# The FFN pre-norm of the next 512 tokens moved into the up-projection loop of the current 512

## The reference, cut to what matters

```python
def rmsnorm(x, g):
    y = x * lax.rsqrt(jnp.mean(x * x, axis=-1, keepdims=True) + EPS)
    return y * g

for l in range(DEPTH):
    h = rmsnorm(x, norm_mix_pre[l])
    proj = h @ w_in[l]
    # retention in chunks of 128 tokens (4 heads) -> y_ret
    # short gated convolution (3 taps)            -> y_sc
    # GLU, convolution of 31 taps, layernorm      -> y_cf
    merged = gates[:, :, 0] * y_ret + gates[:, :, 1] * y_sc + gates[:, :, 2] * y_cf
    x = x + rmsnorm(merged @ w_o[l], norm_mix_post[l])

    h = rmsnorm(x, norm_ffn_pre[l])
    up = causal_dwconv(h @ w_up[l], ffn_conv_w[l])       # 3 taps, per channel
    gate, val = jnp.split(up, 2, axis=-1)
    f = (jax.nn.silu(gate) * val) @ w_down[l]
    x = x + rmsnorm(f, norm_ffn_post[l])
```

## Time and profile before

| | |
|---|---|
| median of 3 runs | 3403.17 us (3396.67 to 3809.15) |
| the profiled execution's own time | 3395.79 us |
| its span, first to last instruction, slowest core (core 6) | 3394.3 us |
| spans of the 8 cores | 3382.3 to 3394.3 us |
| granted TensorE clock, mean over the span | 0.899 to 0.902 |
| PE busy | 2760.2 us, 81% |
| DVE busy | 1414.1 us, 42% |
| ACT busy | 1030.6 us, 30% |
| POOL busy | 151.2 us, 4% |
| DMA queue of POOL, share of the 16 engines | 31.3% |

### The profile page before, as it was taken

The page is one execution under the profiler, slowest core; times in us unless marked ns, Lnnn a source line. Parts: engine busy times, 40 slices in busy tenths (PEclk is TensorE's granted clock), DMA queues, the critical chain, the costliest instruction groups (busy, mean ns, idle before and its releaser), DMA issues.

```text
span 3394.3 us, 41546 instructions; the slowest of 8 cores (3382.3 to 3394.3 us)
## 1 busy us (share of the span) xinstructions
PE 2760.2 (81%) x12476; PEld 1257.4 (37%) x12724; DVE 1414.1 (42%) x4445; ACT 1030.6 (30%) x1825; POOL 151.2 (4%) x290
## 2 busy tenths in 40 slices
PE   3688796697897979898966879777879796979797
PEld 1333343343343434343432324333324343434343
DVE  3423445424454343434343334553334543434343
ACT  1421322422223232323234132323132332323232
POOL 0000000000001000000000000000000010101010
PEclk9899897798898989898977979888989898989898
DMA  6030333030427552525231204231114292626251
GB/s 177 16 54 13 76 66 70 2 67 1 87 49 125 87 87 50 89 49 94 52 72 21 47 13 92 38 72 35 33 37 81 44 167 58 112 51 106 56 100 44
DMA packets 51274, 219.60 MB, mean 65 GB/s; under 512 B 5104, under 2 KB 5360, under 8 KB 43888
## 3 DMA queue, kind: packets, MB, share of 16 engines
q0 software_dynamic: 41184, 187.71, 31.3%
q1 hardware_dynamic: 9872, 29.21, 2.6%
HBM read 396.21 MB, written 8.39 MB: 119 GB/s over the span
## 4 chain that ended last, share of the span: by engine, by line
PE 71%; DVE 11%; issue 7%; ACT 6%; DMA 3%; DVEq 0%; SPq 0%; ACTq 0%; POOLq 0%
PE PSF L402 70%; ACT arena L384 4%; DVE arena L387 2%; DVE arena L396 2%; DVE arena L391 2%; DMA RING<-wst 1%; PE PSB L406 1%; DVE RS L396 1%; ACT HT L384 1%; DVE arena L411 1%; DMA PVt<-pv 1%; DMA out<-X 1%; DVE SMALL L599 1%; ACT SMALL L410 1%; DVE SMALL L411 0%
## 5 line engine op out<-in xcount | busy, mean ns | idle before, releaser
L402 PE MATMUL PSF<-HT,RING 128*128 128x512 bf16 x6016 | 1418.1, 387 | 72.9 <-ACT arena L384 33.0
L384 ACT ACTIVATE arena<-PSF 128x512 bf16<-128x512 f32 (+2 forms) x1024 | 610.2, 597 | 1533.2 <-PE PSF L402 1236.3
L402 PE MATMUL PSF<-arena 128*128 128x512 bf16 (+2 forms) x3796 | 859.9, 372 | 167.3 <-DVE arena L387 68.8
L402 PEld LDWEIGHTS PSF<-HT,RING 128*128 128x128 bf16 x6144 | 608.3, 99 | 825.9 <-issue 130.3
L387 DVE TENSOR_TENSOR arena<-PSF,arena 128x512 f32<-128x512 f32 (+1 forms) x592 | 403.3, 690 | 679.4 <-PE PSF L402 447.4
L402 PEld LDWEIGHTS PSF<-arena 128*128 128x128 bf16 (+1 forms) x3868 | 368.2, 98 | 614.3 <-issue 189.3
L391 DVE TENSOR_SCALAR arena<-CST,PVt 128x128 bf16<-128x128 f32 x1600 | 330.5, 279 | 68.0 <-PE PSF L402 68.0
L406 PE MATMUL PSB<-IDB,arena 128*128 128x128 bf16 x704 | 94.6, 298 | 300.3 <-DVE arena L391 243.9
L356 POOL DMA_DIRECT2D RING<-wst x264 | 139.5, 529 | 3166.6 <-PE PSF L402 1501.1
L399 DVE COPY FH<-arena 128x2 bf16<-128x2 bf16 x352 | 60.5, 172 | 375.0 <-ACT arena L384 373.8
L402 PE MATMUL PSF<-arena,RING 128*128 128x512 bf16 x752 | 196.0, 380 | 0.8
(11 more groups left out here) (49 smaller groups left out, 845.1 us busy)
## 6 DMA issues: line engine op xcount, KB each, us to landing
RING<-wst POOLq DMA_DIRECT2D x192, 512.0 KB, 5.5
RING<-wst POOLq DMA_DIRECT2D x32, 1152.0 KB, 8.3
RING<-wst POOLq DMA_DIRECT2D x24, 1024.0 KB, 7.9
RING<-wst POOLq DMA_DIRECT2D x16, 768.0 KB, 6.4
arena<-wst POOLq DMA_DIRECT2D x22, 512.0 KB, 9.7
X<-x SPq DMA_DIRECT2D x4, 2048.0 KB, 20.6
arena<-rope SPq DMA_DIRECT2D x16, 512.0 KB, 8.5
out<-X SPq DMA_DIRECT2D x4, 2048.0 KB, 7.0
```

Source lines behind the costliest of these rows:

```text
L384: S.op("act", lambda e: e.activation(out=out, in_=in_, func=func, **kw), r, w)
L402: S.pe([(lambda e, o=o, a=a, b=b, s0=s0, s1=s1: e.matmul(o, lhsT=a, rhs=b, start=s0, stop=s1)) for (o, a, b, s0, s1) in specs], r, w)
```

## The change

The diff does these things:

1. `HT` is used as two halves of 512 tokens, in turn: quarter q lies in half q % 2.
2. The FFN's `prenorm` becomes `ffn_stats(q)` (four Squares into a scrap tile `JUNK`, mean and epsilon, Sqrt, reciprocal, results in `PST`) and `ffn_apply(q)`. The latter works in two pairs of token tiles through `HN2`, a buffer of two tiles: two DVE multiplications, then for each of the 8 channel blocks two transposes into a `PSB` bank and one move of 256 columns into `HT`.
3. Quarter 0's stats and apply stand ahead of the loop over quarters. Those of quarter qt + 1 are emitted in quarter qt's up loop, at j = 6 (stats) and j = 13 (apply), each ahead of `up_front(j + 1)`.
4. The arena's push and pop around each quarter are gone, and with them the barrier at each quarter's end; the buffers are allocated once. `slR`, the Silu result, is bf16 instead of fp32.
5. In `ret_front` each PSUM tile has a fixed bank (0: value, 1: gate, 2 and 3: scores, 4 and 5: output, 2 again: the state update) instead of the rotation's next one.
6. The `AR.pop()` and `AR.push()` between the retention and the short convolution are gone, with the barrier.

```diff
-    def pf():
+    def pf(fixed=None):
+        if fixed is not None:
+            return PSF[:, fixed, :], "pf%d" % fixed
...
-                pv_, pvr = pf()
+                pv_, pvr = pf(0)
...
-                pg, pgr = pf()
+                pg, pgr = pf(1)
...
-                psA, psAr = pf()
-                psB, psBr = pf()
+                psA, psAr = pf(2)
+                psB, psBr = pf(3)
...
-                poA, poAr = pf()
-                poB, poBr = pf()
+                poA, poAr = pf(4)
+                poB, poBr = pf(5)
...
-                    pkv, pkvr = pf()
+                    pkv, pkvr = pf(2)
...
-            AR.pop()
             if l == 0 and hf == 0:
                 DBG("ART", ART, ["art0", "art1"])
-            AR.push()
...
+        HN2 = AR.alloc([2, 1024], BF16)
...
+        slR = Rot("sl", [512], BF16)
...
+        def ffn_stats(q):
+            sl_ = (q % 2) * 16
+            for a in range(4):
+                tt = q * 4 + a
+                ACT(JUNK[:], X[:, tt, :], AF.Square, ["x%d" % tt], ["junkp", "fss%d" % (q % 2)],
+                    accum_out=PST[:, sl_ + a:sl_ + a + 1])
+            TS(PST[:, sl_ + 4:sl_ + 8], PST[:, sl_:sl_ + 4], 1.0 / D, EPS, ALU.mult, ALU.add, ["fss%d" % (q % 2)], ["fms%d" % (q % 2)])
+            POW(PST[:, sl_ + 8:sl_ + 12], PST[:, sl_ + 4:sl_ + 8], ["fms%d" % (q % 2)], ["frs%d" % (q % 2)])
+
+        def ffn_apply(q):
+            sl_ = (q % 2) * 16
+            g = q % 2
+            for pair in range(2):
+                for a2 in range(2):
+                    a = pair * 2 + a2
+                    tt = q * 4 + a
+                    TS(HN2[:, a2, :], X[:, tt, :], PST[:, sl_ + 8 + a:sl_ + 9 + a], None, ALU.mult, None,
+                       ["x%d" % tt, "frs%d" % (q % 2)], ["hn2_%d" % a2])
+                for kc in range(8):
+                    p, pr = pb()
+                    TR([(p[:, a2 * 128:(a2 + 1) * 128], HN2[:, a2, kc * 128:(kc + 1) * 128]) for a2 in range(2)],
+                       ["hn2_0", "hn2_1", "idb"], [pr])
+                    dst = HT[:, kc, g * 512 + pair * 256:g * 512 + (pair + 1) * 256]
+                    res = ["ht%d_%d_%d" % (kc, g, pair)]
+                    if kc % 2 == 0:
+                        ACT(dst, p[:, 0:256], AF.Copy, [pr, "pv"], res, scale=PV[:, PV_FFNPRE + kc:PV_FFNPRE + kc + 1])
+                    else:
+                        TS(dst, p[:, 0:256], PV[:, PV_FFNPRE + kc:PV_FFNPRE + kc + 1], None, ALU.mult, None, [pr, "pv"], res)
+
+        ffn_stats(0)
+        ffn_apply(0)
         for qt in range(4):
-            AR.push()
-            HNv = ACTT[:, 0:8, :].rearrange("p a b -> p (a b)").rearrange("p (t d) -> p t d", d=1024)
-            prenorm(l, [qt * 4 + a for a in range(4)], PV_FFNPRE, HT, HNv, lambda i: ["actt%d" % (2 * i), "actt%d" % (2 * i + 1)])
...
+            hg = qt % 2
+            HTq = HT[:, :, hg * 512:(hg + 1) * 512]
+            htr = ["ht%d_%d_%d" % (kc, hg, pr_) for kc in range(8) for pr_ in range(2)]
...
             for j in range(NFF):
                 wd_maybe(j)
+                if qt < 3 and j == 6:
+                    ffn_stats(qt + 1)
+                if qt < 3 and j == 13:
+                    ffn_apply(qt + 1)
                 nctx = up_front(j + 1) if j + 1 < NFF else None
...
-            AR.pop()
         AR.pop()
```

More of the change, by code:

```diff
@@ L321, in build @@
     SM_ = nc.alloc_sbuf_tensor("SMALL", [128, 64], F32)
+    PST = nc.alloc_sbuf_tensor("PST", [128, 32], F32)
+    JUNK = nc.alloc_sbuf_tensor("JUNK", [128, 1024], BF16)
     PSF = nc.alloc_psum_tensor("PSF", [128, 6, 512], F32)
@@ L816, in build @@
         ACTT = AR.alloc([NFF, 512], BF16)
+        HN2 = AR.alloc([2, 1024], BF16)
+        UGR = Rot("ug", [514], BF16)
+        UVR = Rot("uv", [514], BF16)
+        DGF = Rot("dgf", [6, 128], BF16)
+        slR = Rot("sl", [512], BF16)
+        tmpR = {"junk": AR.alloc([512], BF16), "t": Rot("pnt", [512], F32, 2)}
         S.dma("sp", lambda e, l=l: e.dma_start(out=GBC[:], in_=gbc_d[l, 1]), "gbc", writes=["gbc"])
         wd_issued = 0
-        for qt in range(4):
-            AR.push()
-            HNv = ACTT[:, 0:8, :].rearrange("p a b -> p (a b)").rearrange("p (t d) -> p t d", d=1024)
-            prenorm(l, [qt * 4 + a for a in range(4)], PV_FFNPRE, HT, HNv, lambda i: ["actt%d" % (2 * i), "actt%d" % (2 * i + 1)])
[L823 to L827, removed]
+        def ffn_stats(q):
[6 more added lines that the diff above has]
+            POW(PST[:, sl_ + 8:sl_ + 12], PST[:, sl_ + 4:sl_ + 8], ["fms%d" % (q % 2)], ["frs%d" % (q % 2)])
@@ L842, in up_front @@
                 pg_, pgr_ = pf()
-                MM([(pg_, W[:, kc, 0:128], HT[:, kc, 0:512], kc == 0, kc == 7) for kc in range(8)], htr + [wr], [pgr_])
+                MM([(pg_, W[:, kc, 0:128], HTq[:, kc, :], kc == 0, kc == 7) for kc in range(8)], htr + [wr], [pgr_])
                 pv2, pv2r = pf()
-                MM([(pv2, W[:, kc, 128:256], HT[:, kc, 0:512], kc == 0, kc == 7) for kc in range(8)], htr + [wr], [pv2r])
+                MM([(pv2, W[:, kc, 128:256], HTq[:, kc, :], kc == 0, kc == 7) for kc in range(8)], htr + [wr], [pv2r])
                 ACT(ug[:, 2:514], pg_, AF.Copy, [pgr_], [ugr])
@@ L881, in build @@
                 DBG("ACTT", ACTT, ["actt%d" % j for j in range(NFF)])
-            tmpR = {"junk": AR.alloc([512], BF16), "t": Rot("pnt", [512], F32, 2)}
             for a in range(4):
```

## The result

| | before | after |
|---|---|---|
| median of 10 runs | 3402.5 us | 3327.1 us |
| ratio, after to before | | 0.9771 (95%: 0.9753 to 0.9790) |
| span of the profiled execution, slowest core | 3394.3 us | 3323.6 us |
| span of core 6 in both | 3394.3 us | 3320.6 us |
| granted TensorE clock | 0.899 to 0.902 | 0.911 to 0.913 |

The change made the kernel faster by 2.3%; forecast were 3342 us and 1.8%, with a range of 3316 to 3376.

What follows compares the result with a forecast made beforehand. PE, busy 81% of the span, was taken as the bound, with time to gain where it idles or runs at the lower clock. -157.0 + 96.0 + 5.0 - 5.6 = -61.6 us from 3403.2 gave 3342 us, range 3316 to 3376.

Steps and rivals of the forecast that it cites:

- The boundaries: Six quarter ends in the FFN: PE's idle time, transposes and cold matmuls there all go, -157.0 us.
- The stop in step 13: Apply at j = 13 of the up loop: PE loses 12.5 us a quarter to products, transposes and moves (bounds 11.5, 15.1).
- The clock: Up matmuls behind the stop in step 13: lower PE clock loses 2.1 us a quarter (bounds 0 and 2.9).
- The stats: Squares and Sqrt at j = 6 of the up loop: PE held up 1.4 us a quarter (bounds nothing and 4.2).
- the cost in the loop: Moved pre-norm in the up loop: 1.4 + 12.5 + 2.1 = 16.0 us a quarter, times six 96.0.
- Quarter 0: Pre-norm ahead of each layer's quarter loop, now in two pairs: +2.5 us each, +5.0 in all.
- Retention barriers: Barrier between retention and short convolution removed: 1.4 us, four times, -5.6 us.
- Retention chunks: Fixed PSUM banks in the retention: nothing gained; a clock shift of 16 us at most, in either direction.
- the cheaper stop: Rival on the up loop: clock may stay at 1.00, stats may hide; 12.5 us a quarter, 3321 us total; 26%.
- The dearer stop: Rival on the up loop: rounds at 1.52 us and half the stats' upper bound; 20.8 us a quarter, 3371 total; 13%.
- The boundary did not stay in part: Rival at quarter ends: `up_tail(0)` waits behind the last post-norm, 5.4 us each, +32, 3374 us total; 5%.
- The lower clock: Rival, slower than before: after the apply the clock stays at 1.2 GHz for the rest of the up loop; about 3560 us; 3%.

## Why the prediction was nearly right

**The boundaries, -157.0 us.** The mechanism was right, and the gain whole. The six gaps are gone, no wait took their place on PE but the ring's 3.5 us, which the prediction had set to nothing. The rows of all six come to 160.0: the prediction took the slow matmuls from two quarters (2.1 us each; over all six the mean is 2.3) and the transposes from one that took 6.3 us, where two took 6.7.

**The stop in step 13, 12.5 us.** By the rows 12.2, 12.2, 12.0, 12.4, 11.8 and 12.1. The move of 256 columns takes 0.47 us on ACT (0.46 was worked out), a round 1.09 us at the lower clock (1.09) and 0.99 at the higher, the second pair's wait 2.03.

**The clock, 2.1 us.** The clock does fall, but the slow matmuls behind the stop cost 1.4, 1.1, 0.9, 0.5, 1.5 and 1.9 us, 1.2 on average. The mean of the boundaries was too high a stand-in; why the clock comes back sooner here no run shows.

**The stats, 1.4 us.** 0.56 in the trace: in the rows above 0.36 at `up_tail(7)`, where I had 0.5, and 0.20 at `up_front(9)`, where I had 0.9. The Silu behind the stats did not hold the bank for as long as I had put it.

**The mis-sized term** is the cost in the loop, 6 x 16.0 = 96.0. It came to 6 x 13.9 = 83.5 by the rows (12.1 + 1.2 + 0.56), and the run without the apply gives 6 x 13.4 for its part. These 12.5 us are as large as the whole difference between -61.6 and the measured -74 on core 6; the other errors cancel.

**The smaller parts.** Quarter 0: from the last mixing matmul to the first up matmul 25.9 us before and 28.6 after in layer 1, 25.6 and 28.3 in layer 2, so 5.4 us (forecast 5.0). Counted to `up_tail(0)` it is 4.2. Retention barriers 5.7 (5.6). Retention chunks: no gain that can be told from their own movement (nothing). The mixing parts of both layers together are 5.5 us shorter on core 6. The sum by rows: -160.0 + 83.5 + 4.2 - 5.5 + 3.5 = -74.3; the span of core 6 says -73.7.

**The rivals.** Of the cheaper stop (26%) the half on the stats came about; the clock fell. The result, -2.3%, lies between it and the forecast, on the side of 2% to which I had given 0.36; I had held a change within 2% for likelier (0.61). The dearer stop is out: a round took 1.0 to 1.1 us, not 1.52. The boundary did not stay in part, though the same wait is what the barrier brings back (5.39 us, where 5.4 was the price). The lower clock did not last.

What the prediction left out is that the barrier and the pre-norm are not two gains to add: it named the gap's total, not who holds it. The barrier alone, put back, takes the whole net gain.

## What to carry to other kernels

Moving a stage into a loop hid it only on the engines that had slack. On the engine that was the bound, each wait inside the moved block was paid where it stood, since the block's transposes stand ahead of that engine's next matmuls. Ask of the moved block what its longest dependent chain is (products, transposes, moves) and put a loop step between its links: 13.4 us became 1.8. And look for a barrier first: this one held PE for the post-norm's tail (5.4 us) and in layer 2 until the store had landed (13.4 us), and with it in place the moved work brought nothing.

## What the runs showed of the hardware that I had not expected

A group of four 128x128 transposes between two streams of 512-column matmuls at 2.4 GHz cost 0.22 us, and the clock stayed at 1.00. A 2 MB store that took 7.0 us with the other queues still took 19.6 us beside the weight stream (medians of four), yet held PE up for under 4 us in all.
